# Start addresses of the dense products' operands: 32 bytes behind a multiple of 64 for the moving ones, at a multiple of 64 for the weights

## What is computed

```python
def reference(x, ...):
    x = first_block(x, ...)    # hybrid_layer, then rms_norm
    return second_block(x, ...)

def hybrid_layer(x, ...):
    z = rms_norm(x, norm_g) @ w_in
    q, c_kv, q_idx, k_idx, w_idx, g_attn, x_rnn, g_rnn, merge = split_cols(z)
    ...
    y_attn = (o * jax.nn.silu(g_attn)) @ w_attn_proj
    y_rnn = (h * jax.nn.silu(g_rnn)) @ w_rnn_proj
    ...
    return x + mixed @ w_out

def second_block(x, ...):
    proj = rmsnorm(x, attn_norm) @ w_in
    ...
    mixed = sigmoid(gate_a) * (o_a @ w_o_mla) + sigmoid(gate_b) * (o_b @ w_o_moba)
    x = x + mixed @ w_out
    x = x + hierarchical_moe(rmsnorm(x, ffn_norm), ...)
    return rmsnorm(x, final_norm)
```

## Time and profile before

| | |
|---|---|
| median of three runs | 702.66 us (702.53 to 702.69) |
| profiled execution, its own time | 701.36 us |
| its span, first to last instruction | 699.6 us |
| TensorE busy | 657.5 us, 94% |
| weight loads busy | 549.2 us, 79% |
| VectorE, ScalarE, GpSimd busy | 334.3, 326.8, 379.1 us |
| DMA | 181.72 MB, mean 260 GB/s |

### The profile page before, as it was taken

One profiled execution on the slowest core, in us unless ns is written; L12 is line 12 of the kernel. 1 busy time (PEld: TensorE's weight loads), 2 busy tenths in 40 slices (PEclk: granted clock), 3 DMA queues, 4 the chain that ended last, 5 costly groups with the idle time before them and its releaser, 6 DMA issues.

```text
span 699.6 us, 13827 instructions
## 1 busy us (share of the span) xinstructions
PE 657.5 (94%) x5608; PEld 549.2 (79%) x5608; DVE 334.3 (48%) x684; ACT 326.8 (47%) x603; POOL 379.1 (54%) x284
## 2 busy tenths in 40 slices
PE   5999999999999999999999999999999999786894
PEld 4899899999999999998899999999745555343442
DVE  5869623787881247885764555352621221121102
ACT  6566777866553446665357755342311111111004
POOL 3978557798887989999697655784000000000000
PEclk9999999999999999999999999999999999999998
DMA  8875333534436555565356433799999999999994
GB/s 341 324 287 186 121 122 123 169 132 148 154 126 237 181 181 181 181 212 205 127 181 241 129 123 123 305 424 401 360 423 422 420 420 422 420 423 422 422 416 155
DMA packets 27282, 181.72 MB, mean 260 GB/s; under 512 B 3024, under 2 KB 3280, under 8 KB 6864
## 3 DMA queue, kind: packets, MB, share of 16 engines
q1 hardware_dynamic: 26784, 179.74, 67.3%
q10 hardware_dynamic: 432, 1.05, 0.4%
HBM read 179.73 MB, written 1.05 MB: 258 GB/s over the span
## 4 chain that ended last, share of the span: by engine, by line
PE 83%; DMA 10%; DVE 2%; ACT 2%; issue 1%; SPq 0%; POOL 0%; ACTq 0%; DVEq 0%
PE D L517 49%; PE L L998 6%; DMA spare<-w_expert_dram 4%; DMA big<-w_expert_dram 4%; PE L L973 3%; PE QB L1046 3%; PE L L701 2%; PE D L565 2%; PE D L1081 2%; DMA ring<-w_dense_dram 2%; PE TB L710 2%; PE TB L1081 1%; PE L L1007 1%; PE L L673 1%; PE D L569 1%; PE D L548 1%
## 5 line engine op out<-in xcount | busy, mean ns | idle before, releaser
L1584 POOL TENSOR_TENSOR ring_r<-ring,ring_r 128x512 fp32r<-128x512 f32 (+1 forms) x280 | 378.9, 1386 | 100.3 <-ACT ring_r L1170 99.8
L517 PE MATMUL D<-scr_r,ring_r 128*128 128x256 f32 x1104 | 214.1, 289 | 0.0
L1170 ACT ACTIVATE ring_r<-ring 128x1024 fp32r<-128x1024 f32 (+2 forms) x140 | 145.1, 1042 | 92.9 <-PE D L517 81.1
L517 PEld LDWEIGHTS D<-scr_r,ring_r 128*128 128x128 f32 x1104 | 175.6, 191 | 2.4 <-issue 1.6
L517 PE MATMUL D<-hT_r,ring_r 128*128 128x256 f32 x552 | 156.1, 283 | 0.0
L517 PE MATMUL D<-big_r,ring_r 128*128 128x256 f32 x1086 | 134.1, 284 | 1.4 <-POOL ring_r L1584 1.4
L517 PEld LDWEIGHTS D<-big_r,ring_r 128*128 128x128 f32 x1086 | 131.3, 192 | 3.1 <-POOL ring_r L1584 2.1
L517 PEld LDWEIGHTS D<-hT_r,ring_r 128*128 128x128 f32 x552 | 105.7, 192 | 1.1 <-issue 0.7
L1601 DVE SCALAR_TENSOR_TENSOR th<-th,L 64x256 f32<-64x256 f32 x32 | 13.4, 418 | 124.0 <-ACT th L1506 123.5
L1506 ACT ACTIVATE th<-L 64x256 f32<-64x256 f32 x16 | 6.0, 377 | 80.7 <-PE L L998 80.7
L973 PEld LDWEIGHTS L<-wkr,big 128*128 128x128 f32 x240 | 27.9, 191 | 10.6 <-issue 10.6
(11 more groups left out here) (401 smaller groups left out, 1004.6 us busy)
## 6 DMA issues: line engine op xcount, KB each, us to landing
ring<-w_dense_dram SPq DMA_DIRECT2D x69, 1024.0 KB, 4.9
big<-w_expert_dram SPq DMA_DIRECT2D x32, 1024.0 KB, 25.3
ring<-w_expert_dram SPq DMA_DIRECT2D x20, 1024.0 KB, 26.1
spare<-w_expert_dram SPq DMA_DIRECT2D x8, 1024.0 KB, 16.6
wu<-w_expert_dram SPq DMA_DIRECT2D x5, 1024.0 KB, 21.9
small<-w_expert_dram SPq DMA_DIRECT2D x4, 1024.0 KB, 18.6
scr<-w_expert_dram SPq DMA_DIRECT2D x4, 1024.0 KB, 18.5
hT<-w_expert_dram SPq DMA_DIRECT2D x4, 1024.0 KB, 19.4
```

The costliest lines, as they stand in the source:

```text
L517: last = mm(out_, r32(w[i][ws]), r32(x[j][xs_]), start=start and m == 0, stop=stop and m == 2)
L1170: A_(r32(hi_unit(j)[w]), dense_unit(j)[w], ACT.Copy).then_inc(hi_ready, 1)
L1584: last = g.tensor_tensor(r32(w), w, r32(h).bitcast(F32), ALU.subtract)
```

## The change

`sb2` gets the tensor's size in 4-byte words and the place that it shall have within a line of 64 bytes. It allocates up to 8 words more and returns the part that begins at that place; a new view of the old shape is made where the old shape was used. `hT`, `scr`, `big` and `small` are to begin 32 bytes behind a multiple of 64, `ring` and `wkr` at one. No instruction, wait or order is touched.

By the same rule of laying out, the starts become: `ring` 1152 as before; `hT` 50336, `scr` 58528, `big` 68832 (32 behind); `wkr` 66752 (at a multiple). The words that are skipped move what lies behind: `vec`, `cst`, `xT`, `wrt`, `wu`, `root`, `rinv` come to be 32 behind, `attn` and `th` at a multiple; `small` and `spare` stay 32 behind.

```diff
-        def sb2(name, shape):
+        LINE = 64
+
+        def sb2(name, words, line_at):
 
             offset = -(-nc.sbuf_base // 32) * 32
-            t = sb(name, shape)
-            rounded[name] = nc.alloc_sbuf_tensor_at(f"{name}_r", shape, F32R, offset=offset)
-            return t
-
-
-        ring = sb2("ring", [P, RING, 2 * UNIT])
-        hT = sb2("hT", [P, DC, T])
-        scr = sb2("scr", [P, DC, T])
-        wkr = sb2("wkr", [P, DC, 2 * ROPE])
-        big = sb2("big", [P, 18 * 1024 + 512])
+            skip = (line_at - offset) % LINE // 4
+            t = sb(name, [P, skip + words])
+            rounded[name] = nc.alloc_sbuf_tensor_at(f"{name}_r", [P, skip + words], F32R, offset=offset)
+            return t[:, skip:skip + words]
+
+
+        ring = sb2("ring", RING * 2 * UNIT, 0).rearrange("p (a b) -> p a b", a=RING)
+        hT = sb2("hT", DC * T, 32).rearrange("p (c t) -> p c t", c=DC)
+        scr = sb2("scr", DC * T, 32).rearrange("p (c t) -> p c t", c=DC)
+        wkr = sb2("wkr", DC * 2 * ROPE, 0).rearrange("p (c t) -> p c t", c=DC)
+        big = sb2("big", 18 * 1024 + 512, 32)
...
-        small = sb2("small", [P, 5 * 1024])
+        small = sb2("small", 5 * 1024, 32)
```

## The result

The changed kernel takes 698.91 us in the median, beside 702.58 us of the kernel before in the same comparison: a ratio of 0.9948, with a 95% interval of 0.9933 to 0.9964. It is faster by 3.7 us (0.5%), where the forecast said 8.2. The time lies inside the range (692.3 to 699.5), at its slow end.

A forecast was written before the change was run, and what follows sets the result against it. TensorE bounds the dense stage to about 490 us, DMA the end. A gain of 9.7 us less 0.35, 0.25 and 0.9 gives 8.2, so 702.66 becomes 694.5 us; range 692.3 to 699.5.

The forecast's parts named there:

- The two cases: Dense 256-column products: 120.0 ns apart over `big`, `scr`, `hT`, 116.7 over `small`, claimed to follow from start bytes modulo 64.
- The term for `big`: Dense products reading `big`: claimed to gain 3.3 ns each, within at most 9.7 us for all 2952 products.
- GpSimd's rounding: Rival: two GpSimd subtractions per dense unit hold TensorE back, costing 1.6 us up to half the gain; 696 to 700, chance 0.07.
- the plain products: Plain fp32 products (scores, values, experts) get new pairs of places; taken as zero, bounds 1.8 us either way.
- the two attention turns: Second attention, 363 to 441 us: 72 dense products beside TensorE's waits for softmax and copy gain nothing, 0.25 us lost.
- unit starts: First products of 123 dense units are paced by other work or not yet at 120 ns; 7 ns each, 0.9 us lost.
- the stream of transfers: DMA's expert transfers behind the dense stage: claimed to move earlier by 8.2 us and keep their length.
- vb and ukvv: Products with `ring` moving and `scr`, `hT` or `big` as weights: taken as zero, bounds 0.2 us either way.
- The hole ahead of it: DMA's 1.3 us gap at 500 to 505 us, waiting for the transfers' issue; claimed to shrink by half a microsecond.
- 0.35 beside VectorE: From 452.88 to 465.61 us VectorE sets the pace, so 108 products of omla and out2 gain nothing: 0.35 us lost.
- "No change": Rival: `small` is fast for its place at the partition's far end, not its 32 bytes; 702.7 us, chance 0.08.
- "More": Rival: dense products gain twice 3.3 ns, towards the 106.7 ns of the granted clock; about 686 us, chance 0.01.

The follow-up runs named there:

- the kernel with all at 32: Against the changed kernel, `hT`, `scr`, `big` and `small` all start 32 bytes behind a multiple of 128 as seen from `ring`; 695.33 us, ratio 0.9909 to the kernel before.
- the one with three tensors at 192: Against the kernel before, `hT`, `scr` and `big` start 192 bytes from `ring` modulo 256, `small` 32; 691.46 us, ratio 0.9832.

## Why the prediction was wrong

**The two cases.** The failed step is the sentence on the start bytes: `small` "alone is 32 behind" a multiple of 64, and "the kernel before thus already holds both cases". The rows held two start bytes, and the prediction took from them a rule with a period of 64 that they could not show. By that rule `big`, 32 behind a multiple of 64, was like `small`. Its difference to the ring is 96, and 96 costs as much as 0 (119.9 and 119.8 ns). The term for `big`, 1224 products by 3.3 ns or 4.0 us, came out as nothing: 0.03 us was measured, the wrong way. The start bytes of the changed kernel were known beforehand; had the prediction written them as differences to the ring, `big` at 96 and `small` at 160 would have stood there as places without a row, with 0 as a bound of their gain.

That 698.91 us lies inside the range all the same is luck: the slow part of the range was there for GpSimd's rounding and for the plain products, and neither cost anything.

**What held.** For `hT` and `scr` the sum was 1728 x 3.3 = 5.7 us, less the two attention turns (0.25) and their share of the unit starts (0.9 x 1728/2952 = 0.5), 4.9 us; 4.8 was measured. That the dense gain moves the stream of transfers as a whole held too: 4.47 us in the products, 4.51 at the issue.

**Bounds taken as zero.** vb and ukvv lost 0.20 us, the bound that was named and set to zero. `small`, which "stays as it is", went from 32 to 160 and lost 0.14. The stream, "as long", grew by 0.55 us. The hole ahead of it, which was to shrink by half a microsecond, kept its size. Plain products, VectorE and GpSimd stayed, as predicted.

**The sum again.** 8.2 less `big`'s 4.0, plus what had been taken off for `big` (0.35 beside VectorE, 0.37 of the unit starts), less 0.20 and 0.14: 4.6 us at the dense end, 4.47 measured. Less the stream's 0.55, 3.9 to 4.05, as the profiled executions have it (4.0); the medians say 3.7.

**The loss to VectorE.** The change itself never met it, since `big` gained nothing. Where `big` did gain, in the kernel with all at 32, waits took 1.7 us back (0.75 at cq, 0.93 over `big`, half of it at omla's end), where the prediction had 0.35: it saw the stretch at omla's end, though not that the stretch would lengthen by 0.2, and not the start of cq, where TensorE had reached VectorE's work just in time before.

**The rivals.** "No change" was wrong on its reason, since `small` at 0 is slow as well, but what it said holds for 1224 of the 2952 products. That rival leaned on the Trainium skill (TensorE: Matmul & The Clock Gate, "Step-by-step: what each phase is for"): two independent read ports, no cost of loading weights to the product that runs. The runs disagree with the consequence that the prediction drew from this, and say nothing on the ports themselves: moving the ring alone against `small` took that from 116.8 to 119.8 ns. Rounding did not keep TensorE back: among TensorE's waits from 30 to 490 us no view names GpSimd, neither for the changed kernel nor for the one with three tensors at 192. "More" had a chance of 0.01 on the ground that no row stays below 116 ns; other places do.

## What to carry to other kernels

When one case in a trace is faster than another, write down everything that sets the two apart and in which terms (here the difference between two operands' starts, modulo 256, and not one start modulo 64), and price only what the changed kernel puts at a place that a row has shown; the rest gets zero as a bound. When a product of two operands is paced by something finer than its size, sweep the distance between the two buffers, one tensor at a time, and read length over count in the chain. After a gain of some per cent on the bounding engine, look at the work that used to be just in time: it takes part of the gain back.

## What was not expected

- The mean distance between 256-column products depends on the difference of the operands' starts in steps of 16 bytes or less: 119.8 ns at 0, 118.2 at 16, 116.8 at 32, 118.35 at 48, 117.1 at 64, 119.9 at 96, 115.0 at 192.
- At 64 and 192 two steady patterns exist, 113.3 and 117.8 ns, at 16 three (113.3, 116.7 and 118.7), and an unbroken run of products keeps the one that it settled into within its first dozen; what chooses it was not tried.
- The products of 512 columns go another way: with `scr` and `hT` as weights, 228.7 ns where these lie at 0, 228.8 and 229.0 at 192, but 232.7 to 234.1 at 16, 32, 64, 96 and 128.
- With the same dense products, the granted clock fell to 0.50 in the router in four of the kernels and not in the others, which cost 1.25 to 2.9 us.
